# A hybrid retention / attention / mixture-of-experts layer: experts with tokens stationary, weights of an expert in one transfer of 3 MB

## The reference

```python
def _moe(h, w_rg, b_rg, w_re, b_re, w1, w3, w2):
    ...                      # 4 groups x 8 experts; a token takes the best group and 2 experts in it
    comb = jnp.sum(jax.nn.one_hot(e_id, N_EXPERTS) * w_sel[..., None], axis=1)
    a = jnp.einsum('td,edf->tef', h, w1)        # 1024 -> 256
    b = jnp.einsum('td,edf->tef', h, w3)
    hid = jax.nn.silu(a) * b * comb[:, :, None]
    return jnp.einsum('tef,efd->td', hid, w2)   # 256 -> 1024

def _layer(...):
    mod = silu(c) @ w_ada + b_ada               # shifts, scales and gates
    h = rmsnorm(x, n1) * (1 + sc1) + sh1
    ...                                         # retention (4 heads), windowed attention (8 heads), two gates
    x = x + g1 * (merged @ w_o)
    h2 = rmsnorm(x, n2) * (1 + sc2) + sh2
    x = x + g2 * moe(h2)
# then y = rmsnorm(x, final_g)
```

## Time and profile before

| | |
|---|---|
| Time, median of 3 runs | 1479.54 us (1477.16 to 1480.65) |
| Profiled execution: its time, its span | 1479.7 us, 1477.9 us |
| PE busy | 1305.4 us, 88% |
| DVE, ACT, POOL busy | 541.3, 277.6, 121.5 us |
| HBM read, written | 196.59 MB, 33.05 MB |
| First `up` matmul, last `down` ends | 1042.8, 1404.3 us |

### The profile page before, as it was taken

How to read it: one execution, slowest core, us unless ns; L and a number is a source line. 1 busy time by engine, 2 the same in 40 slices (tenths; PEclk the granted TensorE clock), 3 DMA queues, 4 the chain that set the end, 5 groups by cost and what they waited for, 6 DMA issues and landing times.

```text
span 1477.9 us, 19234 instructions
## 1 busy us (share of the span) xinstructions
PE 1305.4 (88%) x7396; PEld 943.8 (64%) x7396; DVE 541.3 (37%) x1299; ACT 277.6 (19%) x618; POOL 121.5 (8%) x167
## 2 busy tenths in 40 slices
PE   3799999999999998999999969992899999999900
PEld 1455555555543567888888858862787888788700
DVE  0355555555556353111111154447111111111147
ACT  0123222222232132111111021110011111111122
POOL 1000000000001000000000001100100000000066
PEclk8799999999999999999999989995899999999955
DMA  8812201220103082111111042225599999999662
GB/s 333 337 72 76 76 18 66 79 73 28 59 9 124 27 308 86 43 43 43 43 43 43 0 185 86 71 74 203 198 343 349 355 347 353 353 351 347 231 260 94
DMA packets 40696, 230.11 MB, mean 156 GB/s; under 512 B 5149, under 2 KB 8157, under 8 KB 27992
## 3 DMA queue, kind: packets, MB, share of 16 engines
q1 hardware_dynamic: 29296, 191.15, 35.5%
q0 software_dynamic: 6176, 21.35, 4.4%
q10 hardware_dynamic: 5192, 17.18, 3.1%
HBM read 196.59 MB, written 33.05 MB: 155 GB/s over the span
## 4 chain that ended last, share of the span: by engine, by line
PE 69%; issue 14%; DMA 6%; POOL 4%; DVE 3%; SPq 2%; ACT 1%; POOLq 0%; ACTq 0%; DVEq 0%
PE p L1730 16%; PE p L1477 11%; PE p L1639 9%; PE psS L1740 7%; PE p L1643 6%; PE p L1666 3%; PE psS L1639 3%; PE psS L1666 3%; DMA out_st_s<-R 2%; PE psS L1643 2%; PE p L1719 1%; SPq L376 1%; POOL R L548 1%; PE psS L1443 1%; DMA R<-V 1%
## 5 line engine op out<-in xcount | busy, mean ns | idle before, releaser
L1477 PE MATMUL p<-R 128*128 128x512 f32 (+1 forms) x576 | 271.5, 601 | 2.0 <-ACT R L616 2.0
L1730 PEld LDWEIGHTS p<-R 128*128 128x128 f32 x2048 | 236.6, 194 | 17.1 <-issue 15.7
L1730 PE MATMUL p<-R 128*128 128x96 f32 x2048 | 236.1, 277 | 1.1 <-DVE R L1340 1.1
L1477 PEld LDWEIGHTS p<-R 128*128 128x128 f32 (+1 forms) x576 | 93.5, 179 | 102.9 <-issue 98.8
L1639 PE MATMUL p<-R_rounded 128*128 128x344 f32 x864 | 145.2, 326 | 4.1 <-issue 4.1
L1639 PEld LDWEIGHTS p<-R_rounded 128*128 128x128 f32 x864 | 139.5, 191 | 6.8 <-issue 4.6
L1347 DVE TENSOR_TENSOR R<-p,R 128x96 f32<-128x96 f32 x64 | 16.5, 258 | 295.0 <-ACT R L832 295.0
L1740 PE MATMUL psS<-R 128*96 128x512 f32 x256 | 115.2, 592 | 0.0
L1150 DVE TENSOR_TENSOR work<-p,work 128x344 f32<-128x344 f32 x36 | 18.6, 517 | 237.5 <-ACT work L769 237.1
L1643 PE MATMUL p<-R 128*128 128x344 f32 x288 | 87.2, 452 | 0.0
L1740 PEld LDWEIGHTS psS<-R 128*96 128x96 f32 x256 | 39.2, 163 | 51.1 <-issue 50.9
(11 more groups left out here) (263 smaller groups left out, 1503.6 us busy)
## 6 DMA issues: line engine op xcount, KB each, us to landing
R<-in_we SPq DMA_DIRECT2D x32, 2048.0 KB, 9.9
R<-in_we SPq DMA_DIRECT2D x32, 1024.0 KB
R<-in_w_ada SPq DMA_DIRECT2D x8, 2048.0 KB, 8.1
y_dram<-R ACTq DMA_DIRECT2D x32, 384.0 KB
R<-in_x SPq DMA_DIRECT2D x18, 512.0 KB, 3.4
R<-in_w_ada SPq DMA_DIRECT2D x8, 1024.0 KB, 12.5
R<-in_w_qkv SPq DMA_DIRECT2D x4, 2048.0 KB, 15.7
R<-in_lift SPq DMA_DIRECT2D x8, 1024.0 KB, 5.0
```

What stands on the lines that cost most here:

```text
L1477: last = mm(pj_bank[h % 2][0:rows, :], hst[:, k, 0:rows], wqh[:, h, k, :], start=k == 0, stop=k == KD - 1)
L1730: last = mm(up_bank[slot][f][:, w * CAP:(w + 1) * CAP], we[slot][:, c0:c0 + P], xgT[:, k, :], start=k == 0, stop=k == KD - 1)
```

## The change

Four things are changed together.

1. **Experts with tokens stationary and split operands.** For each block ACT rounds half of w1/w3 at a time (`round13`, two of 2048 columns) and w2 (`round2`), and DVE subtracts in place (`rest13`, `rest2`). `up` is then 24 matmuls with the 96 tokens stationary and 512 moving columns, and `down` is 12. The hidden rows come out token-major, so they are transposed (`hidden_turn`) and split (`hidden_out`, `hidden_rest`), as are the tokens (`tokens_out`, `tokens_rest`). `down(b-1)` now comes after `up(b)` and `turn(b+1)`. The rounded halves `h13` and `h2w` have one buffer each.
2. **Weights.** One transfer of 3 MB for an expert into one of three slots. The first three are issued at the start; that of block b waits for `s2` of block b-3.
3. **Rows.** Empty places get a row number out of bounds, so gathers skip them. The results are scattered by POOL straight to two rows per token in `y_dram`, and the block of zeros is gone.
4. **Tail.** SP loads the two rows of each token in one contiguous transfer a tile (1 MB). PE weights and adds them with diagonal matrices (`wdiag`: four float32 products of 512 columns a tile), DVE multiplies by the gate out of PSUM and adds x1. POOL has two operations a tile instead of three.

Semaphores are also merged (`c_step`, `smp_turn`, `smp_win`, `route_r`), with the same order of events.

```diff
-            sp.wait_ge(s["yz"], 1)
-            sp.dma_start(y_dram[NE * CAP:, :].rearrange("(p a) (b c) -> p (a b) c", a=ZR, b=2),
-                         yzero.rearrange("p (o c) -> p o c", o=1).to_broadcast([NOVER * CAP // ZR, 2 * ZR, D // 2])
-                         ).then_inc(s["yz_st"], 16)
...
-                sp.dma_start(we[slot][:, 0:4096], A["we"][bass.ds(e, 1), :, 0:4096].rearrange("o p c -> (o p) c")
-                             ).then_inc(s[f"w13_in{slot}"], 16)
-            def weights2(e, slot):
-                sp.dma_start(we[slot][:, 4096:6144], A["we"][bass.ds(e, 1), :, 4096:6144].rearrange("o p c -> (o p) c")
-                             ).then_inc(s[f"w2_in{slot}"], 16)
+                sp.dma_start(we[slot], A["we"][bass.ds(e, 1)].rearrange("o p c -> (o p) c")).then_inc(s[f"we_in{slot}"], 16)
             sp.wait_ge(s["wo_mm"], NT + 1)
             sp.wait_ge(s["m_c"], NT)
             sp.wait_ge(s["lg_r"], NT + 1)
             sp.dma_start(slot_tab, A["slots"]).then_inc(s["stab_in"], 16)
-            for slot in range(2):
+            for slot in range(3):
                 weights(slot, slot)
-                weights2(slot, slot)
-            with sp.Fori(1, NE // 2) as b2:
-                for slot in range(2):
-                    sp.wait_ge(s["s1"], 2 * (2 * b2 + slot - 1))
-                    weights(2 * b2 + slot, slot)
-                    sp.wait_ge(s["s2"], 2 * b2 + slot - 1)
-                    weights2(2 * b2 + slot, slot)
-            sp.wait_ge(s["ov_n"], 1)
+            def refill(b, slot):
+                sp.wait_ge(s["s2"], b - 2)
+                weights(b, slot)
+            with sp.Fori(0, 9) as b3:
+                for r in range(3):
+                    refill(3 * b3 + 3 + r, r)
+            refill(NE - 2, (NE - 2) % 3)
+            refill(NE - 1, (NE - 1) % 3)
...
+            sp.wait_ge(s["y_done"], 1)
+            for t in range(NT + 1):
+                r = P if t < NT else NS
+                sp.dma_start(yg[0:r, t].rearrange("p j c -> p (j c)"),
+                             y_dram[2 * P * t:2 * (P * t + r), :].rearrange("(p j) c -> p (j c)", j=2)
+                             ).then_inc(s[f"yg_in{t}"], 16)
...
+                pool.indirect_dma_start(out=xg[0:CAP, slot], out_offset=None, in_=h2_dram,
+                                        in_offset=bass.IndirectOffsetOnAxis(ap=slotT[:, b:b + 1], axis=0),
+                                        bounds_check=TA - 1, oob_is_err=False).then_inc(s[f"xg_in{slot}"], 16)
+            def scatter_block(b, slot):
+                pool.wait_ge(s["y_e"], b + 1)
+                pool.indirect_dma_start(out=y_dram, in_=yb[0:CAP, slot], in_offset=None,
+                                        out_offset=bass.IndirectOffsetOnAxis(ap=slotY[:, b:b + 1], axis=0),
+                                        bounds_check=2 * TA - 1, oob_is_err=False).then_inc(s[f"y_st{slot}"], 16)
+            pool.wait_ge(s["route_r"], RT["slots"])
             pool.wait_ge(s["h2_st"], 16 * (NT + 1))
+            for b in range(3):
+                gather_block(b, b)
+            pool.wait_ge(s["route_r"], RT["rows"])
             for b in range(NE):
+                if b + 3 < NE:
+                    pool.wait_ge(s["xgT_t"], b + 1)
+                    gather_block(b + 3, b % 3)
                 if b >= 2:
-                    pool.wait_ge(s["xgT_t"], b - 1)
-                gather_block(b, b % 2)
+                    scatter_block(b - 2, (b - 2) % 3)
+            scatter_block(NE - 2, (NE - 2) % 3)
+            scatter_block(NE - 1, (NE - 1) % 3)
...
+            def round13(b, u, slot, n):
+                act.wait_ge(s[f"we_in{slot}"], 16 * n)
+                if not first_block(b):
+                    act.wait_ge(s["u_done"], 2 * (b - 1) + u + 1)
+                nc.scalar.copy(half(h13, u), half(we[slot], u)).then_inc(s["w13_hi"], 1)
+            def round2(b, slot, n):
+                act.wait_ge(s[f"we_in{slot}"], 16 * n)
+                if not first_block(b):
+                    act.wait_ge(s["s2"], b)
+                nc.scalar.copy(h2w, we[slot][:, 4096:6144]).then_inc(s["w2_hi"], 1)
+            def first_block(b):
+                return isinstance(b, int) and b == 0
+            def tokens_out(b):
+                act.wait_ge(s["xgT_t"], b + 1)
+                for j, bk in enumerate((p5, p6)):
+                    nc.scalar.copy(xT_hi[:, 4 * j:4 * j + 4, :], bk[:, 0:4 * CAP].rearrange("p (k t) -> p k t", k=4)
+                                   ).then_inc(s["xhi_r"], 1)
+            def gate(b, slot):
+                act.wait_ge(s["u_done"], 2 * b + 2)
+                nc.scalar.activation(sgh, up_bank[slot][0:CAP, 0:DE], ACT.Sigmoid).then_inc(s["hs"], 1)
+            def hidden_out(b):
+                act.wait_ge(s["hidT_t"], b + 1)
+                nc.scalar.copy(hidT_hi, p2[:, 0:2 * CAP].rearrange("p (f t) -> p f t", f=2)).then_inc(s["hidhi_r"], 1)
+            def rows_back(b, slot, st):
                 act.wait_ge(s["s2"], b + 1)
                 if st is not None:
                     act.wait_ge(s[f"y_st{slot}"], st)
                 nc.scalar.copy(yb[0:CAP, slot].rearrange("p (a c) -> p a c", a=2), psS[0:CAP, :, :]).then_inc(s["y_e"], 1)
-                act.wait_ge(s["y_e"], b + 1)
-                act.dma_start(y_dram[bass.ds(b * CAP, CAP), :], yb[0:CAP, slot]).then_inc(s[f"y_st{slot}"], 16)
-            expert(0, 0, None)
-            expert(1, 1, None)
-            with act.Fori(1, NE // 2) as b2:
-                expert(2 * b2, 0, 16 * b2)
-                expert(2 * b2 + 1, 1, 16 * b2)
+            def expert(b, r, n, n_next, st):
+                slot, before, after = r, (r - 1) % 3, (r + 1) % 3
+                round2(b - 1, before, n[before])
+                hidden_out(b - 1)
+                round13(b + 1, 0, after, n_next)
+                gate(b, slot)
+                tokens_out(b + 1)
+                round13(b + 1, 1, after, n_next)
+                rows_back(b - 1, before, st)
...
+                for j in range(2):
+                    last = nc.scalar.mul(wdiag[:, 2 * t + j, :], ident, wsel[:, 2 * t + j:2 * t + j + 1])
+                last.then_inc(s["wd_r"], 1)
...
+            def rest13(b, u, slot):
+                dve.wait_ge(s["w13_hi"], 2 * b + u + 1)
+                nc.vector.tensor_tensor(half(we_lo[slot], u), half(we[slot], u), half(h13, u), ALU.subtract
+                                        ).then_inc(s["w13_lo"], 1)
+            def rest2(b, slot):
+                dve.wait_ge(s["w2_hi"], b + 1)
+                nc.vector.tensor_tensor(we_lo[slot][:, 4096:6144], we[slot][:, 4096:6144], h2w, ALU.subtract
+                                        ).then_inc(s["w2_lo"], 1)
+            def tokens_rest(b):
                 for j, bk in enumerate((p5, p6)):
-                    nc.vector.tensor_copy(xgT[:, 4 * j:4 * j + 4, :], bk[:, 0:4 * CAP].rearrange("p (k t) -> p k t", k=4)
-                                          ).then_inc(s["xgT_e"], 1)
+                    dve.wait_ge(s["xhi_r"], 2 * b + j + 1)
+                    nc.vector.tensor_tensor(xT_lo[:, 4 * j:4 * j + 4, :], bk[:, 0:4 * CAP].rearrange("p (k t) -> p k t", k=4),
+                                            xT_hi[:, 4 * j:4 * j + 4, :], ALU.subtract).then_inc(s["xT_r"], 1)
             def hidden(b, slot):
-                for f in range(2):
-                    bk = up_bank[slot][f]
-                    dve.wait_ge(s["hs"], 2 * b + f + 1)
-                    nc.vector.tensor_tensor(hid[:, f, :], bk[:, 0:CAP], sgh[:, f, :], ALU.mult).then_inc(s["h_a"], 1)
-                    dve.wait_ge(s["h_a"], 2 * b + f + 1)
-                    nc.vector.tensor_tensor(hid[:, f, :], hid[:, f, :], bk[:, CAP:2 * CAP], ALU.mult).then_inc(s["hid_r"], 1)
-            turn_out(0)
-            with dve.Fori(0, NE // 2 - 1) as b2:
-                for slot in range(2):
-                    hidden(2 * b2 + slot, slot)
-                    turn_out(2 * b2 + slot + 1)
-            hidden(NE - 2, 0)
-            turn_out(NE - 1)
+                bk = up_bank[slot]
+                dve.wait_ge(s["hs"], b + 1)
+                nc.vector.tensor_tensor(hid, bk[0:CAP, 0:DE], sgh, ALU.mult).then_inc(s["h_a"], 1)
+                dve.wait_ge(s["h_a"], b + 1)
+                nc.vector.tensor_tensor(hid, hid, bk[0:CAP, DE:2 * DE], ALU.mult).then_inc(s["hid_r"], 1)
+            def hidden_rest(b):
+                dve.wait_ge(s["hidhi_r"], b + 1)
+                nc.vector.tensor_tensor(hidT_lo, p2[:, 0:2 * CAP].rearrange("p (f t) -> p f t", f=2), hidT_hi, ALU.subtract
+                                        ).then_inc(s["hidT_r"], 1)
...
+            def expert(b, r):
+                before, after = (r - 1) % 3, (r + 1) % 3
+                rest2(b - 1, before)
+                hidden_rest(b - 1)
+                rest13(b + 1, 0, after)
+                hidden(b, r)
+                tokens_rest(b + 1)
+                rest13(b + 1, 1, after)
...
```

(83 more changed lines are left out.)

291 lines of the change are left out of this document (160 added, 131 removed), and 3 rows, old and new, of the table s.

## The result

| | before | after |
|---|---|---|
| time, us (median; range) | 1479.16 (1477.16 to 1480.65) | 1586.14 (1582.91 to 1588.94) |
| ratio, 95% interval | | 1.0723 [1.0696, 1.075] |
| span of the profiled execution, us | 1477.9 | 1586.8 |

A forecast was written before the change was run, and what follows sets the result against it. The wait for each expert's 3 MB load was to bound the kernel: E(31) at 1510.8, 14.1 to `y_done`, 54.0 of tail and 1.8 between span and time give 1581 us, range 1560 to 1605 (chance 0.62).

The forecast's parts named there:

- E(1): Expert stage: the end of PE's round 1, whose last work is `down(0)`; forecast at 1062.3 us.
- landing to PE's first matmul: Expert stage: ACT's cast, DVE's subtraction, DVE work queued next and handovers between a load's landing and PE's start, 5.9 us.
- loss of clock: Start of each pair: PE restarts at half clock after its stall, costing 2.4 us, bounds 0 and 3.2.
- pair of rounds: Expert stage: two experts' rounds close together, then a stall of some 9 us; 29.9 us a pair, 14.95 an expert.
- E(31): Expert stage: the end of PE's round 31, fifteen pairs after round 1; forecast at 1510.8 us.
- the rival with the pace of a queue: Expert loads: the 3 MB transfer takes 9.8 us instead of 11.05, giving 1562 us; chance 0.11.
- The company: Expert loads: one to three gathers and scatters of 0.26 MB meet a transfer and lengthen it by 1.15 us (0.7 to 2.0).
- the heavier rival: Expert stage: more traffic beside the load or longer slow clock, 13.05 and 3.2 us, giving 1606 us; chance 0.09.
- the rival in which the clock holds: Expert stage: PE keeps full clock through the stalls, 15 x 2.4 us less, giving 1545 us; chance 0.12.
- The hidden transfer: Expert stage: loads stay hidden and the rounded matmuls win, a period of 9.5 us, giving 1417 us; chance 0.04.
- The zero store: Before the merge: dropping this store lets lift weights arrive earlier and the clock probably hold, gaining 5.1 us, bounds 0 and 5.1.
- the loop over POOL: Tail tiles: ACT's square and two POOL operations of at most 1.42 us set a period of 4.1 us.

The follow-up runs named there:

- j_quiet: The changed kernel with the gathers of experts 3 to 31 and all scatters bounded to row 0, so they move at most one row: 1541.61 us.
- c_fill: The changed kernel with five float32 matmuls of 512 columns, whose results nothing reads, added on PE after each `down`: 1538.32 us.
- c_fill4: The changed kernel with four float32 matmuls of 512 columns, whose results nothing reads, added on PE after each `down`: 1533.97 us.
- b_own: The changed kernel with the load split: 2 MB (w1, w3) issued once `up` has read its slot, 1 MB (w2) still after `down`: 1430.83 us.
- a_split: The changed kernel with the 3 MB load split into 2 MB (w1, w3) and 1 MB (w2), both still waiting for `s2`: 1539.81 us.

## Why the prediction was right

| step | predicted | measured |
|---|---|---|
| first `up` | 1041.4 | 1039.9 |
| E(1) | 1062.3 | 1061.8 |
| load and SP's issue | 12.4 | 13.3 |
| landing to PE's first matmul | 5.9 | 5.7 |
| PE's round / loss of clock | 9.2 / 2.4 | 9.2 / 2.4 (2.1 to 2.6) |
| pair of rounds, mean of 15 | 29.9 | 30.4 |
| E(31) | 1510.8 | 1518.3 |
| E(31) to `y_done` | 14.1 | 16.5 |
| `y_done` to the span's end | 54.0 | 52.0 |

**The mechanism held in every step of the pair**: the load waits for `down`, ACT's cast stands in program order behind the landing, rounds come in pairs with a stall of 9.2 us, the next load starts at the end of the pair. That the total came so close is in part luck: fourteen pairs of 30.68 us put E(31) 11 us late, and the last pair, whose load is alone (10.4 us), gives 3 of them back.

**The load** came within 0.9 us by two errors against each other. The lone transfer, 11.05 in the sum, is 10.4 (last load) and 10.3 (j_quiet), half way to the rival with the pace of a queue (9.8). The company, 1.15 in the sum, is 2.7. The whole load of 13.15 is thus that of the heavier rival (13.05) and not the 12.2 of the forecast; that rival's loss of clock, 3.2, did not come. The company is what I had named, gathers above all; I had priced it by the bytes of some two meetings, and it cost twice that. The fit in the Trainium skill (DMA: Bandwidth & Descriptors, section "Anatomy of one DMA — SWDGE (gpsimd) path") gives 9.2 us for 3 MB; the page measured it for transfers that GpSimd issues, and the loads here, issued by SyncE, took 10.3 and 13.15.

**The clock** fell at each restart: the first twelve matmuls of a pair take 4.9 to 5.4 us against 2.8. c_fill and c_fill4 show the other side, a clock of 1.00 from 1100 to 1300 us, where c_fill4's stalls are 0.87 to 1.96 us. So the rival in which the clock holds fails for this kernel. The Trainium skill (TensorE: Matmul & The Clock Gate, section "HAM oscillation — how this bites in real kernels") describes a matmul kernel whose matmuls for a tile are shorter than the wait for the next transfer, and which is throttled anew in every round of its loop. This trace agrees on the second part, with the start of each pair at the half clock, though here PE works some 21 us in each pair and stands still for 9.2.

**The hidden transfer**, the rival on the other side, named 1417 us. b_own realises it with another wait: 1430.8. The difference is its price: I had put PE and DVE at 9.5 us as the floor, and once the stock is used up a round takes 10.2.

**The ends.** The zero store was worth 5.0 us by the rows at the merge, where 5.1 stood. `down(31)` at the half clock took 5.42 us where 2.75 stood in the sum, which accounts for the 2.4 us missing before `y_done`. The tail was 2.0 us shorter. Its tiles take 3.65 us in place of 4.1, since POOL's two operations take 0.19 and 0.55 us here, not 1.42 as in the earlier trace rows (timeline of the changed kernel, one tile, the start of the next, and the last operation):

```profile
1565.41 0.19 POOL L601 TENSOR_SCALAR small<-small 128x1 f32<-128x1 f32 x1 [3.04 <-ACT R L948]
1565.68 0.55 POOL L602 TENSOR_TENSOR small<-small,const 128x1 f32<-128x1 f32 x1
...
1569.06 0.19 POOL L601 TENSOR_SCALAR small<-small 128x1 f32<-128x1 f32 x1 [2.83 <-ACT R L948]
...
1580.84 1.27 DVE L1500 SCALAR_TENSOR_TENSOR R<-R,small 8x1024 f32<-8x1024 f32 x1 [0.91 <-POOL small L602]
```

DVE's operations for a tile set the period now, and the loop over POOL that I had taken for the bound is hidden.

**Where the 107 us are.** The fifteen pairs cost 448.5 us in the forecast and 456.5 in the run; in the kernel before, thirty rounds of 11.22 us were 337. This is 120 more; start and tail give some 13 back. Of the 155 us between the changed kernel and b_own, a_split takes away 46 by the first part's earlier landing, and the other 109 hang on the part of the slot that `up` has long read and that still waits for `down`.

## What to carry to other kernels

When transfers are merged, the merged one inherits the latest of their waits and the last of their landings. Write down, for each buffer, the circle "free, issue, land, convert, consume, free" and divide by the rounds that it spans: here 30.4 us for two rounds, against 9.2 us of PE's work in each. It shows the loss although no engine and no queue is near full. Take the load's time from a row with the same company: alone it took 10.4 us, in its circle 13.1. Where PE then waits in each round, the loss of clock comes on top. Filling the gap with matmuls recovers it, and here shortens the load too (48 us in all); mending the wait was worth three times as much.
